# Dealing contraction rows to partitions as chunk*128+partition in a two-block transformer kernel

## The reference, cut to what matters

```python
def hierarchical_moe(h, ...):              # 16 experts of width 512, 2 of 4 in one group per token
    gates = ...                            # router: t @ w_rg + b_rg, t @ w_re + b_re
    for e in range(16):
        hid = silu(t @ w_gate[e]) * (t @ w_up[e])          # [1024, 512] each
        out = out + gates[:, e:e + 1] * (hid @ w_down[e])  # [512, 1024]

def expert_choice_ffn(h, ...):             # 16 experts of width 2048, each takes 32 tokens
    gate, idx = top_k(softmax(h @ w_router).T, 32)
    hid = silu(xe @ w_gate) * (xe @ w_up)                  # xe = h[idx]; [1024, 2048] each
    out = scatter_add(idx, gate * (hid @ w_down))          # [2048, 1024]
```

## Time and profile before

| | |
|---|---|
| median of 3 runs | 2281.72 us (2281.34 to 2281.85) |
| span of the profiled execution | 2284.2 us, 21622 instructions |
| PE busy | 1743.9 us (76%), 8161 matmuls |
| PEld (weight loads) busy | 890.8 us (39%) |
| DVE, ACT, POOL busy | 446.8, 306.1, 106.6 us |
| DMA | 670.59 MB in 203983 packets, mean 294 GB/s |
| chain that ended last | PE 57%, DMA 25%, SP's queue 9%, DVE 4%, issue 2%, ACT 2% |

### The profile page before, as it was taken

How to read it: one execution, slowest core, us unless ns; L and a number is a source line. 1 busy time by engine, 2 the same in 40 slices (tenths; PEclk the granted TensorE clock), 3 DMA queues, 4 the chain that set the end, 5 groups by cost and what they waited for, 6 DMA issues and landing times.

```text
span 2284.2 us, 21622 instructions
## 1 busy us (share of the span) xinstructions
PE 1743.9 (76%) x8161; PEld 890.8 (39%) x8161; DVE 446.8 (20%) x920; ACT 306.1 (13%) x620; POOL 106.6 (5%) x99
## 2 busy tenths in 40 slices
PE   7899999789997799999997655655464656665564
PEld 2674654354443577778653411211121111211121
DVE  5431532422223222112324300000000000000001
ACT  6110222010111222222122100000000000000000
POOL 7000000000000100111010000000000000000000
PEclk9999999889999799999998777878888776778888
DMA  8889344359997343443422599999999999999996
GB/s 276 317 309 362 132 167 147 125 218 418 418 417 288 124 147 111 147 148 134 159 96 74 205 410 409 409 409 409 409 409 410 409 409 409 409 407 409 409 409 256
DMA packets 203983, 670.59 MB, mean 294 GB/s; under 512 B 12484, under 2 KB 15241, under 8 KB 195697
## 3 DMA queue, kind: packets, MB, share of 16 engines
q1 hardware_dynamic: 199376, 657.51, 74.0%
q0 software_dynamic: 3744, 11.11, 1.6%
q10 hardware_dynamic: 768, 0.64, 0.1%
HBM read 661.88 MB, written 7.34 MB: 293 GB/s over the span
## 4 chain that ended last, share of the span: by engine, by line
PE 57%; DMA 25%; SPq 9%; DVE 4%; issue 2%; ACT 2%; POOL 0%; DVEq 0%; ACTq 0%; POOLq 0%
PE psum L846 13%; PE psum L836 11%; DMA hT<-in_w_down 10%; DMA hT<-in_w_gate 9%; SPq L551 8%; PE psum L1324 8%; DMA hT<-in_w_up 6%; PE psum L1144 5%; PE psum L1167 2%; PE psum L1115 2%; PE psum L804 2%; DVE work L176 1%; PE psum L1177 1%; PE psum L1067 1%; PE psum L1260 1%
## 5 line engine op out<-in xcount | busy, mean ns | idle before, releaser
L1324 PE MATMUL psum<-ring,work 128*32 128x512 f32 x2048 | 336.6, 811 | 273.5 <-DMA ring<-in_w_up 114.9
L846 PE MATMUL psum<-ring,hT 128*128 128x512 f32 x672 | 304.9, 600 | 3.2 <-ACT hT L176 2.2
L1324 PEld LDWEIGHTS psum<-ring,work 128*32 128x32 f32 x2048 | 86.6, 143 | 518.4 <-issue 513.4
L836 PE MATMUL psum<-hT,ring 128*128 128x256 f32 x1152 | 277.1, 385 | 1.5 <-DVE hT L176 1.5
L1324 PE MATMUL psum<-work 128*32 128x512 f32 x768 | 165.2, 803 | 131.9 <-DMA hT<-in_w_gate 47.1
L176 ACT ACTIVATE work<-psum 128x512 f32<-128x512 f32 (+3 forms) x151 | 85.4, 565 | 1275.7 <-PE psum L1344 355.7
L836 PEld LDWEIGHTS psum<-hT,ring 128*128 128x128 f32 x1152 | 213.7, 193 | 36.1 <-issue 10.5
L176 DVE TENSOR_TENSOR work<-psum,work 128x512 f32<-128x512 f32 x72 | 49.8, 692 | 730.9 <-PE psum L1324 614.9
L846 PEld LDWEIGHTS psum<-ring,hT 128*128 128x128 f32 x672 | 124.6, 192 | 135.8 <-issue 133.7
L1324 PE MATMUL psum<-hT,work 128*32 128x512 f32 x256 | 164.6, 804 | 0.0
L1324 PEld LDWEIGHTS psum<-work 128*32 128x32 f32 x768 | 42.5, 142 | 249.9 <-issue 249.9
(11 more groups left out here) (319 smaller groups left out, 1500.9 us busy)
## 6 DMA issues: line engine op xcount, KB each, us to landing
ring<-in_w_up SPq DMA_DIRECT2D x128, 1024.0 KB, 18.1
ring<-in_w_gate SPq DMA_DIRECT2D x96, 1024.0 KB, 18.0
ring<-in_w_down SPq DMA_DIRECT2D x96, 1024.0 KB, 18.2
ring<-in_w_in SPq DMA_DIRECT2D x72, 1024.0 KB, 7.2
work<-in_w_gate SPq DMA_DIRECT2D x48, 1024.0 KB, 18.4
work<-in_w_down SPq DMA_DIRECT2D x48, 1024.0 KB, 18.3
ring<-in_w_mod SPq DMA_DIRECT2D x24, 1024.0 KB, 8.8
ring<-in_w_ada SPq DMA_DIRECT2D x24, 1024.0 KB, 7.6
```

The costliest lines, as they stand in the source:

```text
L836: mm = pe.matmul(o[:, wide(j * S, S)], w[:, ch], actT[:, c, :], start=(c == 0), stop=(c == KC - 1))
L846: mm = pe.matmul(o, actT[:, c, wide(t * P, P)], w, start=(c == 0), stop=(c == KC - 1))
L1324: mm = pe.matmul(outs[b][wide(i * CAP2, CAP2), :], lhs(2 * n + c, i), R.slot(l0 + 4 * n + i, (2, width))[:, c, wide(b * BANK, BANK)], star ...
```

## The change

Every contraction over D takes channel c*128+p for chunk c and partition p. The weight views become `(c p)`, and the transposes and gathers read 128 adjacent numbers. The same for the condition vectors, the norm's weight and the routers' weights. Instructions, their order and their waits are as before; only access patterns differ.

```diff
@@ load_chunk
-            src = w.rearrange("(p c) n -> p c n", c=kc)
+            src = w.rearrange("(c p) n -> p c n", c=kc)
@@ MoE loads
-                        moe_loads.append((w.rearrange("e (p c) f -> e p c f", c=KC)[:, :, c0:c0 + 4, :], 2 * p + i, (4, FF), reader))
+                        moe_loads.append((w.rearrange("e (c p) f -> e p c f", c=KC)[:, :, c0:c0 + 4, :], 2 * p + i, (4, FF), reader))
@@ expert-choice loads
-                rows_first = w.rearrange("e (p c) f -> e p c f", c=KC)[:, :, :, wide(fp * 1024, 1024)]
+                rows_first = w.rearrange("e (c p) f -> e p c f", c=KC)[:, :, :, wide(fp * 1024, 1024)]
@@ gpsimd: small_w from w_in (two column ranges), w_router_group, w_router_expert, w_router_2 likewise, and
-            pool.dma_start(ssd_w[:], A["ssd_norm_w"][0].rearrange("(p c) -> p c", c=KC)).then_inc(signal("ssd_w_in"), 16)
+            with nc.allow_non_contiguous_dma(reason="1024 numbers"):
+                pool.dma_start(ssd_w[:], A["ssd_norm_w"][0].rearrange("(c p) -> p c", c=KC)).then_inc(signal("ssd_w_in"), 16)
@@ transpose_tokens
-                            mm = pe.transpose(o[:, wide((c - c0) * P, P)], src[:, t, c::KC], ident)
+                            mm = pe.transpose(o[:, wide((c - c0) * P, P)], src[:, t, wide(c * P, P)], ident)
@@ attention output
-                    mm = pe.transpose(o[:, wide(c * P, P)], o_fox[:, t, c::4], ident)
+                    mm = pe.transpose(o[:, wide(c * P, P)], o_fox[:, t, wide(c * P, P)], ident)
@@ gather
-                        mm = pe.matmul(o[:, wide(i * 4 * width, 4 * width)], h[:, t, c::KC], pick[:, t, 0:4 * width], start=(t == 0), stop=(t == TT - 1))
+                        mm = pe.matmul(o[:, wide(i * 4 * width, 4 * width)], h[:, t, wide(c * P, P)], pick[:, t, 0:4 * width], start=(t == 0), stop=(t == TT - 1))
@@ scalar queue, first loads
-            a.dma_start(cact[:, 0, :], A["c"][0].rearrange("(p c) -> p c", c=KC)).then_inc(signal("c_in"), 16)
-            a.dma_start(cact[:, 1, :], A["c_2"][0].rearrange("(p c) -> p c", c=KC)).then_inc(signal("c_in"), 16)
+            with nc.allow_non_contiguous_dma(reason="2048 numbers"):
+                a.dma_start(cact[:, 0, :], A["c"][0].rearrange("(c p) -> p c", c=KC)).then_inc(signal("c_in"), 16)
+                a.dma_start(cact[:, 1, :], A["c_2"][0].rearrange("(c p) -> p c", c=KC)).then_inc(signal("c_in"), 16)
```

More of the change, by code:

```diff
@@ L659, in _ @@
             with nc.allow_non_contiguous_dma(reason="24 columns"):
-                pool.dma_start(small_w[:, :, 0:HEADS], w_in.rearrange("(p c) n -> p c n", c=KC)[:, :, wide(DT0, HEADS)]).then_inc(signal("dtf_in"), 16)
-                pool.dma_start(small_w[:, :, HEADS:24], w_in.rearrange("(p c) n -> p c n", c=KC)[:, :, wide(F0, FOX_HEADS)]).then_inc(signal("dtf_in"), 16)
+                pool.dma_start(small_w[:, :, 0:HEADS], w_in.rearrange("(c p) n -> p c n", c=KC)[:, :, wide(DT0, HEADS)]).then_inc(signal("dtf_in"), 16)
+                pool.dma_start(small_w[:, :, HEADS:24], w_in.rearrange("(c p) n -> p c n", c=KC)[:, :, wide(F0, FOX_HEADS)]).then_inc(signal("dtf_in"), 16)
             pool.dma_start(small_b[:, 0:HEADS], A["dt_bias"]).then_inc(signal("dtf_in"), 16)
@@ L673, in _ @@
             with nc.allow_non_contiguous_dma(reason="20 columns"):
-                pool.dma_start(small_w[:, :, 0:4], A["w_router_group"][0].rearrange("(p c) n -> p c n", c=KC)).then_inc(signal("router_in"), 16)
-                pool.dma_start(small_w[:, :, 4:20], A["w_router_expert"][0].rearrange("(p c) n -> p c n", c=KC)).then_inc(signal("router_in"), 16)
+                pool.dma_start(small_w[:, :, 0:4], A["w_router_group"][0].rearrange("(c p) n -> p c n", c=KC)).then_inc(signal("router_in"), 16)
+                pool.dma_start(small_w[:, :, 4:20], A["w_router_expert"][0].rearrange("(c p) n -> p c n", c=KC)).then_inc(signal("router_in"), 16)
             pool.dma_start(small_b[:, 0:4], A["b_router_group"]).then_inc(signal("router_in"), 16)
@@ L705, in _ @@
             with nc.allow_non_contiguous_dma(reason="16 columns"):
-                pool.dma_start(small_w[:, :, 0:E], A["w_router_2"][0].rearrange("(p c) n -> p c n", c=KC)).then_inc(signal("router2_in"), 16)
+                pool.dma_start(small_w[:, :, 0:E], A["w_router_2"][0].rearrange("(c p) n -> p c n", c=KC)).then_inc(signal("router2_in"), 16)
             for t in range(TT):
```

## The result

The changed kernel takes 2293.16 us (median of 6 runs, 2287.89 to 2294.30) against 2282.47 us before (6 runs, 2281.34 to 2286.65): ratio 1.0040, 95% interval 1.0029 to 1.0051, so 7 to 12 us slower, 9.1 us by the ratio. Forecast were 5.6 us, within a range of -5 to +16. The profiled execution spans 2292.5 us, 8.3 us more than the one of before.

The account below looks back on a forecast made before the run. Expert choice was taken as DMA-bound, work before 1300 us mostly a PE chain, with PE and DMA level in the MoE. +8.1 - 1.0 - 0.5 - 1.9 - 0.1 + 1.0 = +5.6 us, 2287.3 us; range 2277 to 2298.

Parts of the forecast that it names:

- lead: MoE: the last up loads land 2.5 us before PE needs them, the only cover against a slower load stream.
- MoE gate and up loads: MoE: 2 KB pieces at 390 GB/s make 52 loads 10.6 us later; less 2.5 us of cover, +8.1 us.
- Last MoE gather: MoE: the gather behind the last up load gains 1.0 us from adjacent reads; the first three rounds' gathers gain nothing.
- First gathers: First MoE gather gains 0.5 us, first expert-choice gather 1.9 us (ends 0.5 and 4.4), from contiguous reads.
- Transposes: L826, L1057: nothing for batches behind a norm at clock 0.50; only the merge batch gains, about 0.1 us.
- The cost of a stride: Skill's 16-byte line rule: every transpose would gain too, some 3 us, sum about +3; trace agreed only for gathers.
- First loads: Opening: two condition vectors in 4-byte pieces on ScalarE's queue cost +0.5 us each, +1.0 us; bounds nothing and 10.8 us.
- Opening loads and expert choice: Opening weights keep 2 KB pieces, hidden with 1.4 us to spare; expert-choice gate and up keep 4 KB: no effect.
- A: Rival: piece size costs nothing in the MoE, stream holds 422 GB/s; whole -5.0 us, 2276.7 us; chance 0.15.
- B: Rival: chunks 1 MB apart slow the expert-choice stream, at 386 GB/s +39 us; sum +45, 2327 us; chance 0.04.
- C: Rival: the 4-byte condition loads are dear, +10 for +1.0 us; sum +15, 2296 us; chance 0.11.
- D: Rival: strided reads cost more than counted, in transposes and first gathers; sum -0.5 us, 2281.2 us; chance 0.08.

Follow-up runs that it names:

- moe_8k: Changed kernel with the MoE's gate and up loads and gathers back in the old order (8 KB pieces): 2283.72 us, ratio 0.9999 to the kernel before.
- moe_only: Kernel before with only the MoE part of the change (2 KB gate and up pieces, adjacent MoE gathers): 2295.03 us, ratio 1.0048.
- moe_split: Kernel before, each MoE gate/up load taking every other chunk (2 KB pieces 4 KB apart), gathers still strided: 2294.35 us, ratio 1.0043.
- c_thrice: Changed kernel reading the condition vectors three times (four extra loads of 4-byte pieces): 2295.23 us, ratio 1.0047 to the kernel before.
- moe_stride2: Changed kernel with MoE channels at group*256 + 2*partition + chunk (two 4 KB pieces, gather stride 8 bytes): 2282.91 us, ratio 0.9996 to before.

## Why the prediction was right, point by point

- *The forecast as a whole.* The mechanism held; the forecast of 5.6 us lies below the measured interval (6.6 to 11.6 us), and the term that was too small is that of the MoE loads.
- *What bounds the kernel.* The two plateaus were read rightly. The MoE's chain was unbroken PE work, but its stream had only a few microseconds of lead, and moe_8k, moe_only and moe_split show that the loss comes from there.
- *MoE gate and up loads, +8.1 us.* Measured: the last up job ended at 699.75 us before and ends at 710.50 us, 10.75 us later, of which 0.8 us was there at the first product: +10.0. The step was right and its size a fifth too small. The queue of 2 KB pieces runs at 387 GB/s in the MoE, not the 390 of the one stretch that was taken; that makes the term 9.2 by the same working (at 386 it gives 9.5, not the 9.8 that the prediction has). The last up load lands 12.2 us later than before, counted from the first MoE product, where 387 GB/s gives 11.7; this half a microsecond is not explained. The lead was there as read: 2.4 us between the landing and the last 16 products before, 0.14 after. A round with the lead gone takes 63.85 us (678.06 - 614.21) where 63.5 were worked out.
- *Last MoE gather, -1.0 us.* 7.98 to 7.11 us: -0.87. The other three gained nothing, as said: their time became waiting at L1145.
- *First gathers, -0.5 and -1.9 us.* 10.60 to 9.94 us, and 7.92 to 5.95 us: -0.7 and -2.0. The second is firm: 7.92 to 7.96 us in the three kernels with a strided expert-choice gather, 5.82 to 5.95 in the seven without. Most of it comes from the part at clock 1.00, where the last 3.55 us became 1.69; at 0.50 the gather did some 18 instructions in 4.35 us before and some 20 in 4.24 after. The clock rose earlier in it than was worked out (after 4.2 us, not 5.05), so the hit owes something to luck. The first is not firm: the MoE's first gather takes 8.78 to 9.94 us with adjacent numbers and 10.35 to 10.60 with strided ones, but at one and the same stride of 16 bytes 9.16 and 10.51, by when the clock rises. The gathers inside the expert-choice rounds are shorter too and give nothing under 409 GB/s.
- *Transposes, -0.1 us.* 1.98 us for eight at clock 0.50, no change. The merge batch runs at clock 1.00: its second eight take 1.09 us for 1.16 (their weight loads 0.84 us for 0.97), the -0.1 that was forecast, and its first eight 1.04 us in both kernels.
- *The cost of a stride.* The Trainium skill's page "SBUF — State Buffer" has it, in the part on the DMA port swizzle, that each crossing to a new 16-byte line costs, and that two hits on a line are needed for the full rate. The trace agrees for the gathers: 7.11, 7.11, 7.77 and 7.98 us at 4, 8, 16 and 32 bytes, with the step between 8 and 16. It does not agree with the same note's figure that float32 can be strided by four numbers for free, as that is the 7.77 us; and the 0.21 us between 16 and 32 bytes, where every number is on a line of its own in both, the rule does not give. For the transposes it holds by 0.07 us in eight at clock 1.00 and not at all at 0.50.
- *First loads, +1.0 us.* +0.44 us in the trace; half of it, and too small for the runs to show.
- *Opening loads and expert choice, nothing.* Expert choice at 409 GB/s in both halves. The warning of large powers of two between rows in the Trainium skill, page "DMA: Bandwidth & Descriptors", table of latency and other measured facts, did not bear on this change: 1 MB between the two chunks of a partition costs nothing here, and neither do 256 KB in the MoE (387 GB/s with 256 KB and with 4 KB between pieces).
- *Sum.* By the same terms as measured: +10.0 - 0.9 - 0.7 - 2.0 + 0.4 = +6.8 us. The profiles differ by 8.3 us and the ratio says 9.1, 6.6 to 11.6; of the remaining 1.5 us of the profiles, 1.0 is the lower clock of two batches between the MoE and expert choice. The rest is small beside the 5 us by which the first MoE product moves from profile to profile, so that sum and profiles come so close is in part luck; only the MoE and the expert-choice gather repeat to a tenth of a microsecond.
- *Rivals.* A is refuted by moe_split and by the changed kernel's own 387 GB/s, B by the 409 GB/s, C by the 0.44 us in the changed kernel's own trace and by c_thrice, D by the transposes, which do not gain 0.11 us each at either clock, and by the -2.0 us of the first expert-choice gather, for which D had -4.4.

## What to carry to other kernels

Before reordering which rows go to which partition, look at what one load's piece per partition becomes: with 1 MB loads in a full queue, 8, 4 and 2 KB pieces moved 421, 409 and 387 GB/s here, and the MoE, where compute and loads are level, paid for that at once, however unbroken its chain of compute looked; its cover was the lead of the last load, 2.4 us, not the share of busy time. The order of a contraction need not be all of one kind: dealing rows in runs as long as one load holds (group*512 + 4*partition + chunk) kept the whole piece, and runs of two gave the gather its full rate. A faster operand read gave nothing where TensorE waited for data anyway, and little at clock 0.50 (nothing for the transposes, about a tenth of the pace for the gather); count only the batches on the path.

## What the runs showed of the hardware that was not expected

Strided reads of a stationary float32 operand have their step between 8 and 16 bytes: 32 gather instructions with 256 columns take 7.11 us at 4 and at 8 bytes, 7.77 at 16 and 7.98 at 32. And with the DMA engines full, only the size of the piece made a difference down to 2 KB, not the distance, in all that was tried: 387 GB/s whether the pieces of a partition lie 4 KB or 256 KB apart, and 409 GB/s for pieces of 4 KB 512 KB apart (moe_stride2) or 1 MB apart (expert choice).
